# Turning the modulation vector with a 32-column ones weight in four column tiles and a 32x32 transposition

## The reference

```python
def first_block(x, c, ...):
    c_act = jax.nn.silu(c)                       # (1, 1024)
    for l in range(DEPTH):
        mod = c_act @ ada_w[l] + ada_b[l]        # ada_w[l]: (1024, 6144)
        sh1, sc1, g1, sh2, sc2, g2 = ...         # six pieces of 1024
        h = rmsnorm(x, norm1_g[l]) * (1.0 + sc1) + sh1
        x = x + g1 * token_mix(h, ...)           # HGRN2 + latent attention
        h = rmsnorm(x, norm2_g[l]) * (1.0 + sc2) + sh2
        x = x + g2 * grouped_moe(h, ...)         # 16 experts
    return rmsnorm(x, final_g)

def second_block(x, c, ctx, c_ctx, ada_w, ...):
    for i in range(DEPTH):
        sh1, sc1, g1, sh2, sc2, g2 = adaln(c, ada_w[i], ada_b[i])
        # i == 0 also takes adaln(c_ctx, ...) for the context tokens
        ...                                      # window attention / short convolution
        h = h + g2 * conv_ffn(modulate(...), ffn_w_up[i], ...)
```

## Time and profile before

| | |
|---|---|
| median of 3 executions | 1956.35 us (1954.34 to 1958.11) |
| profiled execution, its own time | 1958.38 us |
| its span in the trace | 1956.6 us |
| mean granted TensorE clock | 0.976 |
| TensorE busy | 1845.9 us, 94% of the span |
| VectorE busy | 909.2 us, 46% |
| ScalarE busy | 371.7 us, 19% |

### The profile page before, as it was taken

The page is one execution under the profiler, slowest core; times in us unless marked ns, Lnnn a source line. Parts: engine busy times, 40 slices in busy tenths (PEclk is TensorE's granted clock), DMA queues, the critical chain, the costliest instruction groups (busy, mean ns, idle before and its releaser), DMA issues.

```text
span 1956.6 us, 46189 instructions
## 1 busy us (share of the span) xinstructions
PE 1845.9 (94%) x21084; PEld 1620.5 (83%) x21084; DVE 909.2 (46%) x1598; ACT 371.7 (19%) x723; POOL 24.5 (1%) x24
## 2 busy tenths in 40 slices
PE   6999988999998999997889998999999989999999
PEld 4788776889997788786889997667888988878899
DVE  3877876200004758765000004675667661134265
ACT  3013242100002022232000004163211110021110
POOL 0000200000000000200000000000000000000000
PEclk8999989999999999998999999999999999999999
DMA  9994447699995672643999994211878563335330
GB/s 357 387 384 179 172 172 303 238 376 408 422 414 209 228 286 104 215 172 133 357 343 413 424 405 167 81 44 44 298 268 296 197 212 129 130 129 172 120 119 24
DMA packets 180616, 466.09 MB, mean 238 GB/s; under 512 B 5152, under 2 KB 55936, under 8 KB 172288
## 3 DMA queue, kind: packets, MB, share of 16 engines
q1 hardware_dynamic: 180192, 463.83, 63.9%
q10 hardware_dynamic: 288, 0.26, 0.0%
HBM read 463.03 MB, written 1.05 MB: 237 GB/s over the span
## 4 chain that ended last, share of the span: by engine, by line
PE 85%; DVE 9%; DMA 2%; ACT 2%; issue 2%; SPq 1%; ACTq 0%; DVEq 0%
PE pair L397 83%; DMA ring<-in_ada_w 2%; DVE AR L1575 2%; PE pair L1045 1%; DVE RST L1630 1%; DVE AR L1814 1%; ACT AR L1290 1%; DVE XH L1575 1%; SPq L288 0%; DVE AR L1824 0%; PE pair L902 0%; DVE AR L1828 0%; DVE XH L1815 0%; DVE AR L1868 0%; DVE AR L1806 0%
## 5 line engine op out<-in xcount | busy, mean ns | idle before, releaser
L397 PE MATMUL pair<-XH,ring 128*128 128x256 f32 (+1 forms) x3328 | 752.6, 387 | 19.7 <-ACT XH L1191 16.1
L397 PEld LDWEIGHTS pair<-XH,ring 128*128 128x128 f32 (+1 forms) x3328 | 630.3, 191 | 126.8 <-issue 31.9
L397 PE MATMUL pair<-AR,ring 128*64 128x88 f32 (+2 forms) x14336 | 699.7, 249 | 25.0 <-issue 20.6
L397 PEld LDWEIGHTS pair<-AR,ring 128*64 128x64 f32 (+1 forms) x14336 | 669.2, 139 | 48.6 <-issue 28.7
L2067 DVE TENSOR_TENSOR AR<-AR,pair 128x352 f32<-128x352 f32 x32 | 16.7, 521 | 411.4 <-PE pair L397 411.4
L1575 DVE SCALAR_TENSOR_TENSOR AR<-ring,CACT,AR 128x512 f32<-128x512 f32 x245 | 184.2, 752 | 8.7
L397 PE MATMUL pair<-AR 128*64 128x128 f32 (+3 forms) x1600 | 132.0, 292 | 8.3 <-ACT AR L1462 3.3
L397 PEld LDWEIGHTS pair<-AR 128*64 128x64 f32 (+3 forms) x1600 | 106.2, 146 | 18.0 <-issue 4.5
L2270 DVE SCALAR_TENSOR_TENSOR AR<-pair,VEC,AR 128x255 f32<-128x255 f32 x88 | 41.9, 476 | 96.0 <-ACT AR L1487 96.0
L1394 ACT ACTIVATE AR<-pair 128x352 f32 (+1 forms) x64 | 26.3, 464 | 309.9 <-PE pair L397 309.9
L1487 ACT ACTIVATE AR<-pair,VEC 128x256 f32<-128x256 f32 x88 | 36.5, 465 | 217.9 <-PE pair L397 217.9
(11 more groups left out here) (271 smaller groups left out, 1196.6 us busy)
## 6 DMA issues: line engine op xcount, KB each, us to landing
ring<-in_ada_w SPq DMA_DIRECT2D x48, 2048.0 KB, 13.1
ring<-in_w_gate SPq DMA_DIRECT2D x32, 2048.0 KB, 10.9
ring<-in_w_up SPq DMA_DIRECT2D x32, 2048.0 KB, 10.7
ring<-in_w_down SPq DMA_DIRECT2D x32, 2048.0 KB, 11.4
ring<-in_ffn_w_up SPq DMA_DIRECT2D x44, 1024.0 KB, 7.6
ring<-in_w_in SPq DMA_DIRECT2D x18, 2048.0 KB, 15.2
ring<-in_ffn_w_down SPq DMA_DIRECT2D x8, 2048.0 KB, 7.9
ring<-in_sc_w_in SPq DMA_DIRECT2D x6, 2048.0 KB, 8.5
```

Of the source, the lines that this page charges most:

```text
L397: return pe.matmul(o, lhsT, rhs, start=start, stop=stop, **kw)
```

## The change

The sum over the partitions changes its operands. The weight is now 32 columns of ones, and `acc` is what moves: for j = 0..3, the 128 columns of `acc` whose number modulo 128 lies in 32j..32j+31. The output is 32 equal rows, on PSUM partitions 32j to 32j+31, which is column tile j of the array. A vector so takes 128 columns of PSUM, where it took 4. VectorE then transposes this [128, 128] into `TURNED` (a part of `RST`) in blocks of 32x32, after which column 32m holds features 128m..128m+127, one per partition, and adds the bias to these four columns. `TURNED` is the same for all jobs, so a job waits for the one before it (`mod_taken`), and the addition waits for the transposition (`settle`).

```diff
@@ -197,7 +197,8 @@
-        FIRST_TURN = [q[:, a:a + 8] for q, a in ((PA, 0), (PA, 512), (PD, 512), (PD, 0))]
+        TURNED = RST[:, S:2 * S].rearrange("p (v n) -> p v n", v=2)
+        FIRST_TURN = [q[:, a:a + P] for q, a in ((PA, 0), (PA, 512), (PD, 512), (PD, 0))]
@@ -402,10 +403,10 @@
                     no = ADA_NO[a, l, k]
                     pe.wait_ge(s["rows_summed"], no + 1)
                     for w in range(n_vec(a, l, k)):
-                        acc = acc_of(a, l, k, w)
-                        for m in range(4):
-                            last = mm(q[:, 8 * n + 4 * w + m:8 * n + 4 * w + m + 1], acc[:, m * P:m * P + P], ones[:, 0:1],
-                                      True, True)
+                        acc = acc_of(a, l, k, w).rearrange("p (m j c) -> p j m c", m=4, j=4)
+                        o = q[:, P * (n + w):P * (n + w) + P]
+                        for j in range(4):
+                            last = mm(o[32 * j:32 * j + 32, :], ones[:, 0:32], acc[:, j, :, :], True, True)
                     done(last)
@@ -1581,8 +1582,15 @@
                 multiplied(CHUNK_OF["ada", last_job])
                 b0 = V_ADAB + 48 * (2 * a + l) + 4 * k
+                if taken[0]:
+                    V.wait_ge(s["mod_taken"], taken[0])
+                taken[0] += 1
                 for v in range(n_vec(a, l, k)):
-                    ins = V.tensor_tensor(MOD[:, a, l, 4 * k:4 * k + 4, v], q[:, 4 * v:4 * v + 4], VEC[:, b0:b0 + 4], ALU.add)
+                    step(V.transpose(TURNED[:, v, :], q[:, P * v:P * v + P]))
+                settle()
+                for v in range(n_vec(a, l, k)):
+                    ins = V.tensor_tensor(MOD[:, a, l, 4 * k:4 * k + 4, v], TURNED[:, v, :].rearrange("p (m c) -> p m c", c=32)[:, :, 0],
+                                          VEC[:, b0:b0 + 4], ALU.add)
                 ins.then_inc(s["mod_taken"], 1)
```

More of the change, by code:

```diff
@@ L1593, in take_all @@
                 for n, job in enumerate(jobs):
-                    take_modulation(*job, q[:, 8 * n:8 * n + 8], jobs[-1])
+                    take_modulation(*job, q[:, P * n:], jobs[-1])
             def modulation(jobs, q):
@@ L1605, in modulation @@
                         sum_rows(*job)
-                        take_modulation(*job, q[:, 8 * n:8 * n + 8], job)
+                        take_modulation(*job, q[:, P * n:], job)
             def coef(a, l, k, last_job):
@@ L1617, in coef @@
                 V.wait_ge(s["coef_ready"], n_coef[0])
-            n_coef = [0]
+            n_coef, taken = [0], [0]
             V.wait_ge(s["cact_ready"], 1)
```

## The result

The changed kernel takes 1939.35 us in the median (1937.96 to 1943.81, 4 executions) against 1955.92 us; the ratio is 0.9918, 95% interval 0.9898 to 0.9938. Measured again, beside other kernels, it is 0.9924 (0.9907 to 0.9941). So 15 to 16.6 us are gone, where 12.0 were forecast; 1939.35 lies inside the range of 1938 to 1952. The profiled execution took 1937.96 us, its span is 1936.2 us.

The account below looks back on a forecast made before the run. TensorE, busy 94% of the span, bounds the kernel, after the DMA queue until about 123 us. Savings of 1.5 + 1.1 + 1.8 + 5.15 + 4.0 = 13.5 us, less 1.5 for the clock, give 12.0: 1944.5 us, range 1938 to 1952.

Parts of the forecast that it names:

- The turn: TensorE's matmuls per job: 0.41 us for one vector, 0.63 for two, saving 0.40 (or 0.50) and 1.08 us.
- The transposition: VectorE's 52 transpositions of [128, 128] from PSUM: 0.35 us each, 18 us in all, mostly where VectorE waits for TensorE.
- The turns before 123 us: First four jobs and all turns up to the first of lat2: 0 saved, as the DMA engines are full.
- The places behind VectorE: Turns bounded by VectorE's chain: new waits of about 1.1 us (wo1, layer 0) and 0.9 us (wo0, layer 1).
- Kept: 1.8 of 3.2 us: Layer 0, bb, wo0, wo1: 1.8 us of the saving stays, since VectorE's four takings delay wo1's second turn.
- kv of layer 1: The pair of turns at kv: 0 saved, since the path runs through ScalarE there (804.43).
- the clock: 1.5 us taken off the 13.5 us sum: half of one 2.8 us clock loss behind the new waits.
- The ups: Second block, up1 to up10: ten single turns at 0.40 us, 4.0 us saved; the pair at up0 gives 0.
- Tiles that don't overlap: Rival: a vector's four matmuls run one after another, 1.06 us for one vector, 1.91 for two; 1963.5 us, chance 0.07.
- The slow transposition: Rival: each taking costs 1.0 us, 0.65 more on seven takings on the path, 4.6 us; 1949 us, chance 0.10.
- More is kept: Rival: TensorE also gains before 123 us and the new waits cost no clock; 19.5 us saved, 1937 us, chance 0.06.
- No change: Rival: clock losses after new waits, up to 2.8 us at four places, and later transitions eat the gain; 1955.5 us, chance 0.07.

Follow-up runs that it names:

- dense3: The changed kernel with each vector's four matmuls issued three times over, same operands and outputs; 1952.9 us, ratio 0.9990 to the kernel before.
- full_width: The changed kernel without column tiles: each of the four matmuls has 128 columns of ones and writes all 128 rows; ratio 0.9998 to the kernel before.
- transpose3: The changed kernel with two more transpositions of the same operands behind each one on VectorE; 1950.55 us, ratio 0.9979 to the kernel before.
- mid_only: The changed kernel with the new form only from lat2 of layer 0 to wo1 of layer 1, first block, old form elsewhere; ratio 0.9947 to the kernel before.

## Why the prediction was right, and what was off

The forecast was on the slow side of what came, by 3 to 4.6 us, with the mechanism as described and some terms off. It isn't a lucky hit, but some terms offset each other.

- **The turn.** Priced at 0.41 and 0.63 us, measured 0.35 and 0.57, plus 0.1 ahead of it for the way into the tiles. The fixed part of 0.20 us stands for both, 0.14 and 0.1. In the ups this is 0.35 us less per chunk (0.40 in the sum): the stage from the turn of up1 to the down product took 147.2 us before and 143.7 after.
- **The transposition.** 316 ns for the 0.35 priced; a single taking holds VectorE 0.35 us longer, a pair 0.90. As a half of its own 2.7 us for 2.45. The Trainium skill (VectorE: "DVE Perf Modes", section "The three transpose paths") gives 311 ns for bf16, and the trace agrees, here with float32.
- **The turns before 123 us.** Called worth nothing, and the start of lat2's features is the same in the mean (122.2 us) with both forms. Lat2's second turn went from 122.82 to 121.91, but in three of four profiles with the old form TensorE came to it without a wait, so the margin by which the DMA queue is the path here is small.
- **The places behind VectorE.** The wait ahead of wo1's second turn (1.00 us) and the one at wo0 of layer 1 (0.85) came as described. Two more weren't named: 0.85 us at wo0 of layer 0, and the 0.23 us for `mod_taken` inside bb of layer 1. From the second turn of bb to the features of wo1 in layer 0, 35.77 us became 34.25: 1.5 us where "Kept: 1.8 of 3.2 us" was forecast, and 0.9 against the mean of the four profiles with the old form (35.2).
- **The term that was put at nothing: kv of layer 1.** "The pair at kv: 0, since the path runs through ScalarE there (804.43)." TensorE runs through there without a wait, and the pair gave its full 1.1 us (3.49 became 2.38, with 28.00 us behind it in both).
- **The term that was mis-sized: the clock.** "From it I take 1.5 us for the clock": the new waits cost no clock at all (14.05 us behind each of the 0.85 us ones, 14.08 behind the 1.00), while the wait that was already there, ahead of hi in layer 1, costs 2 us less. Without that term the sum was 13.5 us. With the 2 us, the 1.1 at kv and 0.5 less in the ups it is 16.1, where 15 to 16.6 were measured.
- **By stage.** Layer 0: 4.4 in the sum, 5.4 measured as the difference of two pairs of profiles, 4.3 with four of the old form. Layer 1: 5.15 in the sum, 8.1 and with four profiles of each form 8.6 measured, with 2 us of the difference at hi and 1.1 at kv. The ups: 4.0 in the sum, 3.5 by the turns and 3.8 as a stage. The expert stages have no change in them and differ by more than these errors.
- **The rivals.** Tiles that don't overlap: refuted by dense3, and full_width shows that it would have cost the whole gain (0.9998, where the rival had 7 us more than before; the transpositions, 2.45 us, and the slower turns, 29 x 0.08 = 2.3 us, are about what hi and up0 lost less at the lower clock, 1.4 and 2.6 us). The slow transposition: refuted by its 316 ns, though transpose3 shows that its price was set too low: 0.7 us more for each vector cost 11 to 12 us, where the rival charged 4.6 for 0.65. "More is kept" was half right: the new waits cost no clock, but nothing came from before 123 us. "No change" fell with the same waits.

## What to carry to other kernels

A sum over partitions whose output is narrow should be in the moving operand, with a 32-column ones weight, and its parts spread over the four column tiles: four float32 matmuls of 128 columns then take the time of one, 0.22 us, and without the tiles the exchange of the operands gave nothing. Before counting such a gain, cut the schedule into the places where TensorE is waited for and those where a transfer or VectorE comes last; here the first 12 of 52 turns were worth nothing that could be seen, and from bb to wo0 of layer 0 each instruction added on VectorE or taken from it showed in full. That the chain passes through another engine at a place doesn't make TensorE's time there free, as kv of layer 1 showed: look whether TensorE waits. Where an effect is 0.2%, compare stages as well as totals, over several profiles: the stages that no edit touches moved by up to 6 us.

## What the runs showed of the hardware

- At hi of layer 1, behind a wait of 2.2 to 2.8 us, 1.7 to 3.4 us were lost at the lower granted clock in five profiles of five with the old turn; with column tiles, behind waits of 2.5 to 3.8 us, the loss was 0 in four profiles of eight and 1.7 in the others. At bb of layer 0 both forms lost time in every profile, 2.5 to 3.8 us and 1.4 to 2.8.
- At wo0 of layer 0, waits of 0.76 to 1.81 us left the 64 records behind them at 14.05 us (granted clock 1.00 behind the 1.81, in mid_only); two waits of 1.03 and 2.05 us with one vector's turn between them did not (15.74 us at 0.89, in transpose3).
- 64 full-width records of 256 columns take 13.9 us ahead of full-width matmuls and 14.0 ahead of matmuls in column tiles (32 or 64 columns wide): 0.1 us for the way into the tiles.
- VectorE transposes [128,128] float32 from PSUM in 316 ns, from SBUF in 311, and [128,256] from PSUM in 450.
